# Rotary embedding in a decoder step: the exchange of head halves by DMA instead of matrix products

## The chip, the cores and the metric

One core of one Trainium2 chip runs the whole program. The metric is the device time of one execution in microseconds (us), the median of the runs shown; lower is better.

## The reference, cut to what matters

Two layers of a decoder are computed for 256 prompt tokens and 32 sample tokens (8 sequences of 4), 288 token columns in all, fp32 throughout. A layer is a half-step FFN, a mixing block of three branches (spatial gating, block-sparse attention, memory attention) that all read one combined projection, and a second half-step FFN. The change concerns the queries and keys of the block-sparse attention, which are rotated by position before use: 8 heads of 64 channels, each head split in two halves of 32.

```python
def rope(x, pos):
    hd = x.shape[-1]
    half = hd // 2
    inv = ROPE_THETA ** (-jnp.arange(half, dtype=jnp.float32) * 2.0 / hd)
    ang = pos.astype(jnp.float32)[:, None] * inv[None, :]
    cos = jnp.cos(ang)[None, :, None, :].astype(x.dtype)
    sin = jnp.sin(ang)[None, :, None, :].astype(x.dtype)
    x1, x2 = x[..., :half], x[..., half:]
    return jnp.concatenate([x1 * cos - x2 * sin, x2 * cos + x1 * sin], axis=-1)
...
    h = xn @ w_in
    a_u, a_v, b_q, b_k, b_v, c_q, gates = jnp.split(h, IN_SPLITS, axis=-1)
    q = rope(b_q.reshape(heads), pos)
    k = rope(b_k.reshape(heads), pos)
```

## The kernel before

**Layout and stages.** Activations lie transposed: channels on the 128 partitions, in chunks, and the 288 tokens along the free dimension. Queries and keys have 512 channels each, four chunks of 128x288, so a chunk holds two heads, and a half of a head is a block of 32 partitions. Every weight matrix is streamed from HBM in tiles of 256 columns, in four buffers (two weight slots s of two halves h). ScalarE rounds a loaded half to the fp32r high part (`hi`, L928), VectorE subtracts to get the low part (`lo`, L1303), and TensorE multiplies high by high, high by low and low by high (`tile`, L450, and `part`, L474), three products per chunk and 128 rows. SP issues the weight loads in order; each waits until the low part of the buffer's former contents is done (L1807, L1857).

**The order of the work** is written out by hand for each engine; engines meet only at semaphores, and each engine's queue runs in order. Two result buffers (s = 0 and 1) in PSUM are copied out by ScalarE (`take`, L956), which counts in `evac`; four more banks, numbered by `bank_schedule` (L155), carry transposes and small products.

**The query phase.** TensorE computes the query projection (two tiles at L609 and L617, put by ScalarE into `work[:, 4:6]` and `work[:, 6:8]`, L1089), then the gating values (L622 to L633). VectorE multiplies the queries by the cosine (L1494). Between the halves of the next tile TensorE multiplies each query chunk by a fixed 128x128 matrix `swap` that exchanges the halves of a head with a sign (`rotate`, L569 to L574, called at L623, L624, L627, L628). VectorE multiplies the product by the sine and adds it (`rotate`, L1473 to L1481), then builds block-diagonal queries for the sample group (`own_queries`, L1483) and the block diagonal of the spatial weights (L1504), with the low part of one weight half between the first and the last two rotations (L1497) and two more behind (L1509, L1510).

**The key steps.** 16 steps (L740) transpose four cached key pages each (`page_turn`, L636), with half a projection tile in between, and multiply them by the sample queries (`quad_scores`, L642). GpSimd issues the page loads, four pages (a quad) per step and three quads ahead (`load_quad`, L1923; the loop L1951); between quads it adds squares of the gating values for a layer norm (L1955, L1958), whose sums TensorE takes in steps 1 and 3 (L699 to L705). Transposed pages are copied out by ScalarE (pages 0 and 2) and VectorE (pages 1 and 3). The new keys are projected in steps 0 to 3 and copied out by ScalarE in steps 2 and 4 (`taken`, L1130); VectorE multiplies them by the cosine in steps 3 and 5 (L1591) and rotates them in steps 4 and 6 (L1598, L1602), for which TensorE has two more pairs of `swap` products (L706 to L709). The array `u_T` (`u_t`) is free until ScalarE fills it in steps 6 and 8. The program of GpSimd is written out for both layers.

## Time and profile before

| what | value |
|---|---|
| time, median of 3 runs | 1634.37 us (1634.26 to 1634.77) |
| the profiled execution: time, span | 1636.47 us, 1634.5 us |
| granted TensorE clock, mean of the span | 0.994 |
| DMA traffic | 316.78 MB, 194 GB/s on the mean |

The profile is of one execution. PE is TensorE, PEld its weight loads, DVE is VectorE, ACT ScalarE, POOL GpSimd, SP SyncE; an L number is a line of the kernel. A row of a timeline gives start, length (both us), engine, line, operation, output <- inputs, and how many such instructions follow one another; in brackets, how long the engine had been idle and who ended that. Products overlap in TensorE's pipeline, so a product's length is longer than its share of the time, and start times are the better measure. An fp32 product appears as two instructions.

### The profile page before, as it was taken

Reading aid. Unit: us, or ns where it says so; the run is one execution under the profiler, and the core shown is the slowest. Engines: PE = TensorE matmul, PEld = TensorE weight load, DVE = VectorE, ACT = ScalarE, POOL = GpSimd, SP = SyncE. Lnnn points to the kernel's source line nnn. Section 1 sums busy time; section 2 is a strip of 40 time slices with the busy share of each in tenths; the row PEclk is TensorE's granted clock in tenths of the full one; section 3 lists DMA queues with packets and bytes.
Section 4 is the critical chain, followed back from the end, with each engine's and each line's share of the span. In section 5 each row is a group of like instructions: output and inputs, shape, how many; then the busy total and the mean of one; then the engine's idle time right before and its main releaser. Section 6 shows DMA issues by size and latency. Waiting matters only on the chain.

```text
span 1634.5 us, 34371 instructions
## 1 busy us (share of the span) xinstructions
PE 1602.3 (98%) x13085; PEld 1524.9 (93%) x13085; DVE 938.7 (57%) x1230; ACT 815.8 (50%) x1075; POOL 214.5 (13%) x350
## 2 busy tenths in 40 slices
PE   7999999999999999999999999999999999999996
PEld 6999999998778999999999999999977889999995
DVE  5555556675655566555565555657565556655555
ACT  6756445444635454434476654444455544544343
POOL 1000020332432010000000000113234300100000
PEclk9999999999999999999999999999999999999998
DMA  7555467766876455555555545767678845655552
GB/s 232 157 174 163 145 208 235 255 229 206 278 276 210 145 188 166 165 170 165 169 173 176 155 154 173 264 209 242 217 234 293 269 149 177 190 156 167 162 163 91
DMA packets 253548, 316.78 MB, mean 194 GB/s; under 512 B 12952, under 2 KB 229232, under 8 KB 253424
## 3 DMA queue, kind: packets, MB, share of 16 engines
q1 hardware_dynamic: 225008, 225.87, 44.4%
q0 software_dynamic: 25632, 83.91, 15.0%
q10 hardware_dynamic: 2784, 5.39, 1.0%
q8 instruction: 73, 1.20, 0.3%
q14 instruction: 51, 0.42, 0.1%
HBM read 309.35 MB, written 5.77 MB: 193 GB/s over the span
## 4 chain that ended last, share of the span: by engine, by line
PE 92%; DVE 2%; issue 2%; ACT 1%; DMA 1%; POOL 0%; ACTq 0%; POOLq 0%; SPq 0%; DVEq 0%
PE res L466 44%; PE res L547 17%; PE res L486 16%; PE bank L560 6%; PE bank L648 2%; PE sums L823 2%; PE bank L769 1%; DMA page<-in_cache_v 1%; PE bank L574 0%; PE sums L509 0%; PE bank L795 0%; PE bank L791 0%; POOL work L1904 0%; DVE wlo L1307 0%; DMA xrow<-in_x_prompt 0%
## 5 line engine op out<-in xcount | busy, mean ns | idle before, releaser
L1307 DVE TENSOR_TENSOR wlo<-wraw,whi 128x1024 fp32r<-128x1024 f32 (+1 forms) x452 | 522.4, 1174 | 395.6 <-ACT whi L933 394.3
L933 ACT ACTIVATE whi<-wraw 128x1024 fp32r<-128x1024 f32 (+1 forms) x452 | 443.8, 994 | 279.1 <-PE res L547 143.8
L466 PE MATMUL res<-norm_hi,whi 128*128 128x288 f32 x1632 | 486.1, 298 | 4.7 <-DVE wlo L1307 4.5
L466 PE MATMUL res<-norm_lo,whi 128*128 128x288 f32 x1632 | 483.1, 296 | 0.0
L466 PE MATMUL res<-norm_hi,wlo 128*128 128x288 f32 x1632 | 481.5, 295 | 0.0
L466 PEld LDWEIGHTS res<-norm_hi,whi 128*128 128x128 f32 x1632 | 307.0, 188 | 5.4 <-issue 4.7
L466 PEld LDWEIGHTS res<-norm_hi,wlo 128*128 128x128 f32 x1632 | 308.5, 189 | 0.0
L466 PEld LDWEIGHTS res<-norm_lo,whi 128*128 128x128 f32 x1632 | 307.4, 188 | 0.2
L547 PE MATMUL res<-h_hi,whi 128*128 128x288 f32 x704 | 209.0, 297 | 0.0
L547 PE MATMUL res<-h_lo,whi 128*128 128x288 f32 x704 | 208.1, 296 | 0.0
L547 PE MATMUL res<-h_hi,wlo 128*128 128x288 f32 x704 | 207.5, 295 | 0.0
L486 PE MATMUL res<-norm_hi,whi 128*128 128x288 f32 x544 | 170.8, 314 | 0.0
L1904 POOL TENSOR_TENSOR work<-work 128x576 f32<-128x576 f32 x21 | 36.5, 1738 | 1006.8 <-ACT work L972 1006.6
L486 PE MATMUL res<-norm_lo,whi 128*128 128x288 f32 x544 | 160.5, 295 | 0.0
L486 PE MATMUL res<-norm_hi,wlo 128*128 128x288 f32 x544 | 160.4, 295 | 0.0
L547 PEld LDWEIGHTS res<-h_hi,wlo 128*128 128x128 f32 x704 | 132.7, 188 | 0.0
L547 PEld LDWEIGHTS res<-h_lo,whi 128*128 128x128 f32 x704 | 132.3, 188 | 0.0
L547 PEld LDWEIGHTS res<-h_hi,whi 128*128 128x128 f32 x704 | 132.1, 188 | 0.0
L486 PEld LDWEIGHTS res<-norm_hi,whi 128*128 128x128 f32 x544 | 102.5, 188 | 16.3 <-issue 16.1
L1107 ACT ACTIVATE kT<-bank 128x512 f32<-128x512 f32 x80 | 47.8, 597 | 123.3 <-PE bank L560 123.3
L486 PEld LDWEIGHTS res<-norm_lo,whi 128*128 128x128 f32 x544 | 102.7, 189 | 0.2
L486 PEld LDWEIGHTS res<-norm_hi,wlo 128*128 128x128 f32 x544 | 102.3, 188 | 0.0
(209 smaller groups left out, 2130.1 us busy)
## 6 DMA issues: line engine op xcount, KB each, us to landing
wraw<-in_ffn_w SPq DMA_DIRECT2D x244, 512.0 KB, 4.2
wraw<-in_w_in SPq DMA_DIRECT2D x96, 512.0 KB, 4.8
page<-in_cache_k POOLq DMA_DIRECT2D x128, 256.0 KB, 4.6
page<-in_cache_v POOLq DMA_DIRECT2D x128, 256.0 KB, 5.0
wraw<-in_ffn_w SPq DMA_DIRECT2D x32, 384.0 KB, 3.0
wraw<-in_w_mem_kv SPq DMA_DIRECT2D x16, 512.0 KB, 3.4
page<-in_cache_mem_k POOLq DMA_DIRECT2D x32, 256.0 KB, 4.7
page<-in_cache_mem_v POOLq DMA_DIRECT2D x32, 256.0 KB, 3.5
```

Of the source, the lines that this page charges most:

```text
L466: mm = pe.matmul(res[:, 2 * s + c, 0:n], w_, m_, start=h == 0 and k == 0 and i == 0, stop=h == 1 and k == kh - 1 and i == 2)
L486: mm = pe.matmul(res[:, 2 * s + c, 0:T], w_, m_, start=h == 0 and k == 0 and i == 0, stop=h == 1 and k == kh - 1 and i == 2)
L547: mm = pe.matmul(res[:, 2 * ps + c, 0:T], w_, m_, start=part == 0 and h == 0 and k == 0 and i == 0, stop=part == 2 and h == 1 and k == kh ...
L560: mm = pe.transpose(d, i_, ident[0:i_.shape[0], 0:i_.shape[0]])
L648: mm = pe.matmul(out(bb), q_[:, c, bb, :], kTb[bb][:, c, :], start=c == 0, stop=c == 3)
L769: mm = pe.matmul(bk(nm)[:, qt * 256:(qt + 1) * 256], lhs, rhs, start=True, stop=True)
L823: mm = pe.matmul(bk(nm)[32 * bb:32 * bb + 32, :], PT[:, j, 32 * bb:32 * bb + 32], page[slot(V0 + v, bb)][:], start=j == 0, stop=j == 7)
L933: act.activation(whi[u][:, 0:kh, :], wraw[u][:, 0:kh, :], ACT.Copy).then_inc(hi_done[u], 1)
L1107: act.activation(kTb[bb][:], bk(f"{name}_{bb}")[:, :].rearrange("p (c m) -> p c m", c=4), ACT.Copy)\
L1307: dve.tensor_tensor(wlo[u][:, 0:kh, :], wraw[u][:, 0:kh, :], whi[u][:, 0:kh, :].bitcast(F32), ALU.subtract)\
L1904: a = pool.tensor_tensor(work[:, 0:2, :], work[:, 0:2, :], work[:, 2 * g:2 * g + 2, :], ALU.add)
```

## The change

The matrix `swap`, its eight products per layer, their banks and the VectorE operations on them go. The sine table gets the sign (minus in the first half of a head). GpSimd has a function `exchange(n)` for the two halves of the queries (n = 0, 1) and of the keys (n = 2, 3): it waits for ScalarE's copy of that projection tile, and for the keys until VectorE has read the array's former contents, and then issues four DMAs that copy two chunks of `work` into `u_t`, each of the four blocks of 32 partitions from the block beside it in its head. Each DMA moves 32 partitions x 2304 B. Exchanges 0 and 1 stand before the loads of page quad 3, exchange 2 before quad 6 (and before the addition that is issued there), exchange 3 before quad 8. VectorE waits for all four DMAs of an exchange (`ld_half`), multiplies the exchanged two chunks by the sine in one operation, and adds them in another. The cosine product of the queries is cut into two halves, the first of which moves ahead of the last low part of the pair before. The first low part of the key phase, `lo(0, 0, 8, 1)`, moves behind the block diagonals. ScalarE's wait at step 10 becomes waits at steps 6 and 8, before it overwrites `u_t`.

```diff
@@ -47,8 +47,8 @@
 UP = FF // W
 
 
-C_ID, C_ONE, C_EPS, C_SWAP = 0, 128, 256, 264
-C_COS, C_SIN = C_SWAP + 128, C_SWAP + 128 + T
+C_ID, C_ONE, C_EPS, C_COS = 0, 128, 256, 264
+C_SIN = C_COS + T
 C_CAUSAL = C_SIN + T
 C_NEWMASK = C_CAUSAL + 512
 C_TRIL = C_NEWMASK + 64
@@ -67,17 +67,12 @@
     p = np.arange(P)
     c[:, C_ID:C_ID + P] = np.eye(P)
     c[:, C_ONE:C_ONE + P] = 1.0
-    for m in range(P):
-        if m % HD < HD // 2:
-            c[m + HD // 2, C_SWAP + m] = -1.0
-        else:
-            c[m - HD // 2, C_SWAP + m] = 1.0
     pos = np.concatenate([np.arange(SEQ), np.tile(PAST + np.arange(DEC_T), DEC_B)]).astype(np.float32)
     half = HD // 2
     inv = np.float32(10000.0) ** (-np.arange(half, dtype=np.float32) * np.float32(2.0) / np.float32(HD))
     ang = pos[None, :] * inv.astype(np.float32)[p % half][:, None]
     c[:, C_COS:C_COS + T] = np.cos(ang.astype(np.float64))
-    c[:, C_SIN:C_SIN + T] = np.sin(ang.astype(np.float64))
+    c[:, C_SIN:C_SIN + T] = np.sin(ang.astype(np.float64)) * np.where(p % HD < half, -1.0, 1.0)[:, None]
     key = np.arange(SEQ)
     for qt in range(2):
         c[:, C_CAUSAL + 256 * qt:C_CAUSAL + 256 * qt + 256] = np.where(key[None, :] <= p[:, None] + P * qt, 0.0, NEG)
@@ -129,7 +124,7 @@
 PAIRS = 56
 RES = 48
 SUMS = 5
-STEPS = 51
+STEPS = 56
 HEADS = 12
 KSTEPS = 16
 GATE_STEPS = 12
@@ -156,8 +151,8 @@
 
     pro = [(f"in{t}_{q}", q) for t in range(3) for q in range(2)] + [("gainT", 2)]
     layer = [(f"mt{f}", f % 3) for f in range(4)] + [("mk0", 0), ("mk1", 1), ("wmT", 2), ("mv0", 0), ("mv1", 1)]
-    layer += [("rotq0", 0), ("rotq1", 1), ("rotq2", 0), ("rotq3", 1), ("rep", 2)]
-    side = {4: ["rotk0", "rotk1"], 6: ["rotk2", "rotk3"], 8: ["vn0", "vn1"], 9: ["vn2"], 10: ["sgu0", "sgu1"],
+    layer.append(("rep", 2))
+    side = {8: ["vn0", "vn1"], 9: ["vn2"], 10: ["sgu0", "sgu1"],
             11: ["sgu2", "sgu3"], 12: ["k0", "k1"], 13: ["k2", "v2"], 14: ["pT0_0", "pT1_0"], 15: ["v0", "v1"]}
     for i in range(KSTEPS):
         layer += [(f"kT{i}_{bb}", bb % 2) for bb in range(4)] + [(nm, b) for b, nm in enumerate(side.get(i, []))]
@@ -307,7 +302,6 @@
 
     ident = cst[:, C_ID:C_ID + P]
     ones = cst[:, C_ONE:C_ONE + P]
-    swap = cst[:, C_SWAP:C_SWAP + P]
     epsc = cst[:, C_EPS:C_EPS + 1]
 
 
@@ -370,6 +364,7 @@
     ld_gain = sem("ld_gain")
     ld_x = [sem(f"ld_x{i}") for i in range(3)]
     ld_page = sem("ld_page_ids")
+    ld_half = [sem(f"ld_exchanged_{n}") for n in ("q0", "q1", "k0", "k1")]
     ld_sw = sem("ld_sgu_w")
     ld_sb = sem("ld_sgu_b")
     out_mem, out_vn, out_k, out_v, out_y = (sem(n) for n in ("out_mem", "out_vn", "out_k", "out_v", "out_y"))
@@ -566,14 +561,6 @@
             b = bk(name)
             transposes(name, (L,), [src[:, c, c0:c0 + m] for c in range(4)], [b[0:m, c * P:(c + 1) * P] for c in range(4)])
 
-        def rotate(L, which, c):
-
-            name = f"rot{which}{c}"
-            free(name, L)
-            o = 4 if which == "q" else 0
-            pe.matmul(bk(name)[:, 0:T], swap, work[:, o + c, :], start=True, stop=True).then_inc(filled_of(name), 1)
-
-
         pe.wait_ge(ld_const, 16)
         for t in range(3):
             pe.wait_ge(ld_x[t], 16)
@@ -619,13 +606,7 @@
                 rows(f"mv{t}", L, work, t)
 
 
-            part(0, 0, 8, normed)
-            rotate(L, "q", 0)
-            rotate(L, "q", 1)
-            part(0, 1, 8, normed)
-            pe.wait_ge(evac[1], r[1].at())
-            rotate(L, "q", 2)
-            rotate(L, "q", 3)
+            tile(0, 8, normed)
             wait(empty("wmT", L))
             free("rep", L)
             pe.matmul(bk("rep")[0:NS, 0:16].rearrange("p (g i) -> p g i", g=4), cst[:, C_REP:C_REP + NS],
@@ -677,7 +658,7 @@
                 nm = f"newS_{G}"
                 if G == 0:
                     pe.wait_ge(sum_read, nsum.at(1))
-                    pe.wait_ge(rot_ready, L * 8 + 8)
+                    pe.wait_ge(rot_ready, L * 4 + 4)
                 free(nm, L)
                 for c in range(4):
                     for bb in range(4):
@@ -703,10 +684,6 @@
                 elif i == 3:
                     pe.wait_ge(ch_added, L * 2 + 2)
                     sum_channels(lnsq)
-                elif i in (4, 6):
-                    pe.wait_ge(evac[(i - 4) // 2], r[(i - 4) // 2].at(-1 if i == 4 else 0))
-                    rotate(L, "k", i - 4)
-                    rotate(L, "k", i - 3)
                 elif i == 8:
                     pe.wait_ge(vn_ready, L + 1)
                     rows("vn0", L, gv, 0)
@@ -1037,7 +1014,7 @@
                     split_high(g, lambda k: slice(G_FFN1 + k, G_FFN1 + k + 1))
             hi(s, h, 8, 0)
             square(i)
-        act.dma_start(cst[:, C_SWAP:C_ALL], A["const"][:, C_SWAP:C_ALL]).then_inc(ld_rest, 16)
+        act.dma_start(cst[:, C_COS:C_ALL], A["const"][:, C_COS:C_ALL]).then_inc(ld_rest, 16)
 
         with repeat(act, DEPTH, {cur: PAIRS, r[0]: RES, r[1]: RES, nsum: SUMS, nf: 4, soft_n: HEADS,
                                  silu_n: 2 * UP, xr: 8}) as L:
@@ -1139,9 +1116,8 @@
                     act.activation(lnsq[:], gv[:], ACT.Square, scale=SGU ** -0.5).then_inc(xc_sq, 1)
                 hi(u // 2, u % 2, 4 if i > 12 and u >= 2 else 8, 1)
                 key_copy(f"kT{i}", 2, i)
-                if i == 10:
-                    wait(fill("rotq3", L))
-                    act.wait_ge(rot_ready, L * 8 + 4)
+                if i in (6, 8):
+                    act.wait_ge(rot_ready, L * 4 + i // 2)
                 if i in taken:
                     take(*taken[i])()
                 if u == 3:
@@ -1461,24 +1437,27 @@
             for g in (1, 2, 3):
                 normal_low(g)
             pair(FULL)
-            pair(FULL)
+            cosb = cst[:, C_COS:C_COS + T].unsqueeze(1)
+
+            def queries(s):
+                dve.wait_ge(evac[s], r[s].at(3))
+                step(dve.tensor_tensor(qk[:, 2 * s:2 * s + 2, :], work[:, 4 + 2 * s:6 + 2 * s, :], cosb.broadcast_to([P, 2, T]),
+                                       ALU.mult))
+            pair(FULL, None, lambda: queries(0))
 
 
             wait(fill("wmT", L))
             tril = cst[:, C_TRIL:C_TRIL + P].unsqueeze(1).broadcast_to([P, 4, P])
             dve.tensor_tensor(wmT[:], bk("wmT")[:, :].rearrange("p (g i) -> p g i", g=4), tril, ALU.mult)\
                 .then_inc(emptied_of("wmT"), 1)
-            cosb = cst[:, C_COS:C_COS + T].unsqueeze(1)
-
-            def rotate(which, c):
-                nm, o = f"rot{which}{c}", 0 if which == "q" else 4
-                wait(fill(nm, L))
-                tmp = rtmp[c % 2]
-                if o + c >= 2:
-                    dve.wait_ge(rot_ready, L * 8 + (o + c - 1))
-                dve.tensor_tensor(tmp[:], bk(nm)[:, 0:T], cst[:, C_SIN:C_SIN + T], ALU.mult).then_inc(emptied_of(nm), 1)
-                wait(empty(nm, L))
-                dve.tensor_tensor(qk[:, o + c, :], qk[:, o + c, :], tmp[:], ALU.add).then_inc(rot_ready, 1)
+
+            def rotate(n):
+
+                half, two = u_t[:, n % 2 * 2:n % 2 * 2 + 2, :], qk[:, 2 * n:2 * n + 2, :]
+                dve.wait_ge(ld_half[n], L * 64 + 64)
+                sinb = cst[:, C_SIN:C_SIN + T].unsqueeze(1).broadcast_to([P, 2, T])
+                step(dve.tensor_tensor(half, half, sinb, ALU.mult))
+                dve.tensor_tensor(two, two, half, ALU.add).then_inc(rot_ready, 1)
 
             def own_queries(G):
                 for c in range(4):
@@ -1489,16 +1468,11 @@
                                               1.0, None, ALU.mult)
                 i.then_inc(qbd_ready, 1)
 
-            dve.wait_ge(evac[0], r[0].at(3))
-            dve.wait_ge(evac[1], r[1].at(3))
-            step(dve.tensor_tensor(qk[:, 0:4, :], work[:, 4:8, :], cosb.broadcast_to([P, 4, T]), ALU.mult))
-            rotate("q", 0)
-            rotate("q", 1)
-            lo(0, 0, 8, 1)
-            rotate("q", 2)
-            rotate("q", 3)
+            rotate(0)
+            queries(1)
             step(dve.memset(qbd[:], 0.0))
-            dve.wait_ge(rot_ready, L * 8 + 4)
+            rotate(1)
+            dve.wait_ge(rot_ready, L * 4 + 2)
             own_queries(0)
             wait(fill("rep", L))
             for g in range(4):
@@ -1506,6 +1480,7 @@
                 msk = cst[0:NS, C_BD:C_BD + NS].rearrange("p (b i) -> p b i", b=DEC_B)
                 i = dve.tensor_tensor(bd[:, g, :].rearrange("p (b i) -> p b i", b=DEC_B), src, msk, ALU.mult)
             i.then_inc(emptied_of("rep"), 1)
+            lo(0, 0, 8, 1)
             lo(0, 1, 8, 1)
             lo(1, 0, 8, 1)
             r[0].n += 4
@@ -1597,12 +1572,10 @@
                                            cosb.broadcast_to([P, 2, T]), ALU.mult))
                 elif i == 4:
                     block_scores(0)
-                    rotate("k", 0)
-                    rotate("k", 1)
+                    rotate(2)
                 elif i == 6:
                     step(dve.tensor_tensor(gv[:], gv[:], rstd[:].unsqueeze(1).broadcast_to([P, 4, T]), ALU.mult))
-                    rotate("k", 2)
-                    rotate("k", 3)
+                    rotate(3)
                 elif i == 7:
                     for k in range(4):
                         a = dve.tensor_scalar(gv[:, k, :], gv[:, k, :], gains[:, ds(L * 4 + (G_LNG + k), 1)],
@@ -1623,7 +1596,7 @@
                     dve.wait_ge(ld_sb, L * 16 + 16)
                     dve.wait_ge(evac[0], r[0].at(2))
                     dve.wait_ge(evac[1], r[1].at(2))
-                    dve.wait_ge(rot_ready, L * 8 + 8)
+                    dve.wait_ge(rot_ready, L * 4 + 4)
                     spatial(0)
                     spatial(1)
                 elif i == 11:
@@ -1822,7 +1795,7 @@
                 nk = DOWN_NK[part]
                 load(t % 2, wt[w2][L][:, 8 * part:8 * part + nk, g * W:(g + 1) * W], nk)
 
-        sp.dma_start(cst[:, 0:C_SWAP], A["const"][:, 0:C_SWAP]).then_inc(ld_const, 16)
+        sp.dma_start(cst[:, 0:C_COS], A["const"][:, 0:C_COS]).then_inc(ld_const, 16)
         sp.dma_start(xrow[0][:], A["x_prompt"][0, 0:P, :]).then_inc(ld_x[0], 16)
         sp.dma_start(xrow[1][:], A["x_prompt"][0, P:2 * P, :]).then_inc(ld_x[1], 16)
         sp.dma_start(xrow[2][0:NS, :], A["x_sample"].rearrange("b t d -> (b t) d")).then_inc(ld_x[2], 16)
@@ -1948,7 +1921,23 @@
                     e = slot(quad, bb)
                     pool.dma_start(page[e][:], src).then_inc(page_loaded[e], 16)
             add_squares()
+
+            def exchange(n):
+
+                s, c = n % 2, 4 - n // 2 * 4 + n % 2 * 2
+                pool.wait_ge(evac[s], L * RES + MIX_TILES + n // 2 * 2)
+                if n >= 2:
+                    pool.wait_ge(rot_ready, L * 4 + n - 1)
+                for p0 in range(0, P, HD // 2):
+                    p1 = p0 ^ (HD // 2)
+                    pool.dma_start(u_t[p0:p0 + HD // 2, 2 * s:2 * s + 2, :], work[p1:p1 + HD // 2, c:c + 2, :])\
+                        .then_inc(ld_half[n], 16)
             for quad in range(QUADS):
+                if quad == 3:
+                    exchange(0)
+                    exchange(1)
+                if quad in (6, 8):
+                    exchange(quad // 2 - 1)
                 if quad == 4:
                     pool.wait_ge(evac[1], L * RES + MIX_TILES + 1)
                     pool.wait_ge(out_v, L * 32 + 16)
```

## Rows read from the trace of the kernel before

**Rows 1.** Busy time of each engine, share of the span, instructions.

```profile
PE 1602.3 (98%) x13085; PEld 1524.9 (93%) x13085; DVE 938.7 (57%) x1230; ACT 815.8 (50%) x1075; POOL 214.5 (13%) x350
```

**Rows 2.** The chain that ended last, shares of the span by engine.

```profile
PE 92%; DVE 2%; issue 2%; ACT 1%; DMA 1%; POOL 0%; ACTq 0%; POOLq 0%; SPq 0%; DVEq 0%
```

**Rows 3.** TensorE's waits, 240 to 420 us: for whom, total us, times, longest.

```profile
PE bank L648 <- DVE scores L1527: 0.4, 1, 0.4
```

**Rows 4.** Line 574, the rotation products: lengths in ns, first and last start.

```profile
L574 PE MATMUL bank<-work,consts x32: 405/406/407, 274.1 to 1130.1; 128*128 128x288 f32 x32
```

**Rows 5.** Timeline of TensorE at the first pair of rotation products.

```profile
273.99 0.29 PE L486 MATMUL res<-norm_hi,wlo 128*128 128x288 f32 x1
274.12 1.13 PE L574 MATMUL bank<-work,consts 128*128 128x288 f32 x4
...
275.23 0.29 PE L486 MATMUL res<-norm_lo,whi 128*128 128x288 f32 x1
275.36 0.29 PE L486 MATMUL res<-norm_hi,wlo 128*128 128x288 f32 x1
```

**Rows 6.** Timeline of TensorE, second pair and first page transposes.

```profile
278.28 1.13 PE L574 MATMUL bank<-work,consts 128*128 128x288 f32 x4
279.35 0.24 PE L631 MATMUL bank<-sgu_wT,consts 128*32 128x16 f32 x2
...
286.01 1.04 PE L560 MATMUL bank<-consts,page 128*128 128x128 f32 x8
...
288.46 1.04 PE L560 MATMUL bank<-consts,page 128*128 128x128 f32 x8
```

**Rows 7.** Timeline of TensorE, key steps 2 and 4.

```profile
301.60 1.04 PE L560 MATMUL bank<-consts,page 128*128 128x128 f32 x8
...
304.15 1.08 PE L648 MATMUL bank<-kT,q_blockdiag 128*32 128x128 f32 x32
...
314.73 1.04 PE L560 MATMUL bank<-consts,page 128*128 128x128 f32 x8
...
318.26 1.08 PE L648 MATMUL bank<-kT,q_blockdiag 128*32 128x128 f32 x32
```

**Rows 8.** Page loads: a burst of four from 308.9; then 262 to 420 us.

```profile
L1949 POOL DMA_DIRECT2D page<-in_cache_k x4: 536/536/553, 309.0 to 310.6; - x4
...
DMA to landing us min/median/max: 2.8/4.5/6.4
...
DMA to landing us min/median/max: 2.7/4.2/8.5
```

**Rows 9.** Timeline of GpSimd, key steps 0 to 3.

```profile
287.25 1.13 POOL L1949 DMA_DIRECT2D page<-in_cache_k  x2 [41.76 <-PE bank L560]
...
302.84 1.13 POOL L1949 DMA_DIRECT2D page<-in_cache_k  x2 [1.34 <-PE bank L560]
307.67 1.42 POOL L1958 TENSOR_TENSOR ln_square<-ln_square 128x576 f32<-128x576 f32 x1 [3.70 <-ACT ln_square L1139]
```

**Rows 10.** Timeline of ScalarE, query phase.

```profile
270.27 0.65 ACT L960 ACTIVATE work<-res 128x576 f32<-128x576 f32 x1 [2.08 <-PE res L466]
...
283.07 1.06 ACT L933 ACTIVATE whi<-wraw 128x1024 fp32r<-128x1024 f32 x1 [2.04 <-PE res L466]
```

**Rows 11.** Timeline of VectorE, query phase and key steps 3 and 4.

```profile
273.04 0.68 DVE L1469 TENSOR_TENSOR sgu_wT<-bank,consts 128x512 f32<-128x512 f32 x1
...
283.63 1.45 DVE L1487 TENSOR_SCALAR q_blockdiag<-qk_T 64x16 f32<-64x16 f32 x8
285.12 0.47 DVE L1507 TENSOR_TENSOR sgu_blockdiag<-bank,consts 32x32 f32<-32x32 f32 x4
285.52 2.33 DVE L1307 TENSOR_TENSOR wlo<-wraw,whi 128x1024 fp32r<-128x1024 f32 x2
...
310.69 0.74 DVE L1596 TENSOR_TENSOR qk_T<-work,consts 128x576 f32<-128x576 f32 x1
...
317.13 0.69 DVE L1529 TENSOR_REDUCE stat<-scores 128x2 f32<-128x512 f32 x1
```

## Prediction

> **What bounds the kernel now.** I read the busy shares first: TensorE is busy for 98% of the span [rows 1], no other engine for more than 57%. Busy alone proves nothing, so next the chain that ended last: 92% of it is TensorE, and VectorE, ScalarE and the DMAs share some 4% [rows 2]. Then TensorE's own waits, in the stretch of layer 0 that holds all four pairs of rotation products: the longest is 0.4 us, behind a VectorE read of scores [rows 3]. So every microsecond taken off TensorE's stream there comes off the time, until another engine falls so far behind that TensorE waits for it. The rest of the working is about that "until".
>
> **What goes: the products.** Line 574 stands with 32 instructions [rows 4]: each of the 16 fp32 products is two of them, and they come in pairs of products, four pairs in a layer, eight in all. Their 406 ns overlap in the pipeline, so the price is read from start times. At the first pair the last column product before it starts at 273.99, the pair at 274.12, and the stream is back in its step of 0.13 from 275.23 on [rows 5]; without the pair the instruction of 275.23 would start at 274.12 + 0.13 = 274.25. A pair costs 0.98, a third of it the slow change back. Behind the second pair stands another fp32 product (L631), which starts 1.07 later than the pair [rows 6]. For the key pairs I compare two steps: from the second page transposes to the scores a step without any extra product takes 304.15 - 301.60 = 2.55, one with a rotation pair 318.26 - 314.73 = 3.53 [rows 7]. Again 0.98. Sum: 8 x 0.98 = **7.8 us**; with 1.07 for the two pairs before L631 it would be 8.0. That the step without products runs at 2.55 with no wait also says that the engines around it can follow the shorter step.
>
> **What comes: 32 DMAs on GpSimd's queue.** An exchange is four DMAs of 32 partitions x 2304 B (74 KB), four exchanges in a layer. Issuing: four page loads in a row cost GpSimd 0.54 each [rows 8], so an exchange is 2.1 us of GpSimd and 16 issues are 8.6 us in a layer. What is queued behind them there:
> - The exchanges of the queries come before the loads of page quad 3. GpSimd has sat idle for 41.76 us before these [rows 9], waiting for the first page transposes; both exchanges lie inside, so nothing behind them moves.
> - The first key exchange comes after quad 5 and before the addition L1958, whose sum TensorE multiplies in step 3. Quad 5 is out at 302.84 + 1.13 = 303.97, the addition starts at 307.67, having waited 3.70 for ScalarE [rows 9]: 2.1 us of issuing fit, with 1.5 to spare. The second comes after quad 7, and GpSimd then waits for transposes again.
>
> Landing is the number that the trace does not have: nothing copies SBUF to SBUF here. The nearest rows are those four page loads in one burst on the same queue, 256 KB each: 2.8 to 6.4 us, median 4.5. The fastest page of this phase took 2.7 us, the slowest 8.5 [rows 8]. I take **4.5** (same queue, same burst of four, with more bytes than here), and keep 2.7 and 8.5 as ends.
>
> **Who waits for the landing.** Only VectorE, in order, and only one of the four exchanges is tight: the second half of the queries. Its source is ScalarE's copy that ends at 270.27 + 0.65 = 270.92 [rows 10], before any product that goes, so this time stays. GpSimd issues from 271.0, the fourth DMA at 272.7; landed at 277.2. VectorE meanwhile masks the spatial weights until 273.7, rotates the first half (landed long before; two operations of 128x576 at 0.74 each [rows 11]) until 275.2, does the cosine product of the second half and the clearing, and then waits until 277.2. Behind that wait on VectorE are the rotation (1.5), the own queries (1.45), the block diagonals (0.47) and three low parts of weights at 1.17 [rows 11], of which the first has moved from before the second half of the queries to behind the block diagonals; the last also needs ScalarE's high part, which ends at 283.07 + 1.06 less the 2.0 that TensorE is ahead by then, 282.1 [rows 10]. So the low parts end at 280.6 + 3.5 = 284.1.
> When does TensorE need that? Its first page transposes move from 286.01 to 284.0, the next pair from 288.46 to 286.45 [rows 6], and the fourth page goes into the bank that VectorE's copy of the second page empties, some 0.5 behind that. With the copy at 0.7, VectorE must be free of the low parts by 286.2: 2.1 us to spare, or a landing at 279.3, which is 6.6 us after the fourth issue. 4.5 is free, so is the 6.4 of the burst; at 8.5 the landing is at 281.2, 1.9 late in a layer, **3.8 us** in two. A landing faster than 4.5 gains nothing, since then ScalarE's high part is last.
> The low part that moved also releases a weight load on SP: it ends at 280.6 + 1.2 = 281.8, and ScalarE takes that buffer's next contents only in key step 1, behind the transposes of 286.45, so the load has more than 5 us. The key exchanges are easy: issued by 304.1 in the new times, landed by about 308; VectorE reaches the first key rotation when its block scores end, 317.13 + 0.69 - 2.0 = 315.8 [rows 11].
>
> **Edits at nothing.** VectorE's own work: per layer 17 operations go and 10 come, over the same 5,760 columns (1152 + 16 x 288 against 10 x 576), beside TensorE throughout. The cosine product of the first queries goes into a gap where VectorE waits for ScalarE before the last low part. ScalarE's wait in step 10 becomes waits in steps 6 and 8 on rotations that VectorE ends two steps earlier; if one were late, the activation of that step and the high part of the next would queue behind it. SP's first constant load keeps its size, ScalarE's gets 64 KB smaller. The 2.4 MB of exchanges stand against 316.78 MB moved.
>
> **Sum.** 7.8 off, nothing back. The profiled execution has a span of 1634.5 and a time of 1636.47, 2.1 above the median of the runs; I take the difference from the median: 1634.37 - 7.8 = **1626.6**.
>
> **A rule of the skill that speaks against the change.** The burst row says that DMAs of one queue overlap: four issued within 2.1 us, and the slowest landed 6.4 after its issue [rows 8]. The Trainium skill, "DMA: Bandwidth & Descriptors", section "Rules for kernel authors", says of two transfers to disjoint partition halves "Don't bother — they serialize", and would have one transfer over all partitions. By the fit that the page has in its section "Anatomy of one DMA — SWDGE (gpsimd) path" (2.0 us and the bytes at 436 GB/s; an estimate of 2.2 for 74 KB) four in a row would land 8.7 after the first issue, at 279.7, 0.4 late in a layer, and the sum would be 7.0: 1627.4. No run here shows an exchange yet.
>
> **The rivals.**
> - *Late landing, chance 0.10.* The second query exchange meets the two 512 KB writes of the memory keys and values and the weight loads, and lands like the slowest page. For: ScalarE issues these writes just behind the copy that releases the exchange. Against: the burst stayed at 6.4. Price 3.8: 1630.4.
> - *Serial exchanges, slower, chance 0.05.* The four DMAs go one at a time, each with a whole landing: 4 x 4.5 = 18 after 271.0 is 289.0, 9.7 later than free. VectorE stands at the second query rotation, TensorE at the first kT bank. Twice 9.7 less 7.8 is 11.6: 1646. If the key rotations were held too (18 after 302.0 is 4 past 315.8), it would be more. It becomes a loss once the landing is 3.9 past 279.3, at 283.2, 12 us after the first issue. Against: the burst row.
> - *Nothing gained, chance 0.08.* Another chain sets the pace of the steps (page, transpose, copy, scores), and the time freed turns into TensorE waits: 1634.4. For: two copies per step sit close behind the transposes. Against: rows 7, a step without products at full pace.
>
> **How the numbers follow.** The forecast has the remaining 0.77. Its own spread: a vanished wait of 0.4 in each layer and 1.07 for the L631 pairs would bring 1625.6, less some noise 1625.2. Upwards the range takes in the late landing with a little room: 1631.0. A measurement of this kernel can tell about 0.2%, 3.3 us, from no change; forecast and late landing are faster (0.87, less 0.01 for a hold that I don't see: 0.86), nothing gained is the same (0.08), serial exchanges and that 0.01 are slower (0.06).
>
> **What would show it.** Right: no line 574, the key steps 4 and 6 at 2.55 from transposes to scores, no new TensorE wait on VectorE's kT copy between the query phase and step 1, exchanges landing 3 to 6 us after issue, VectorE idle for about 1 us before the second query rotation. Wrong: VectorE idle there for over 3 us and TensorE waiting at the first kT banks (late or serial), TensorE waiting for the sum of L1958 (issuing dearer than 0.54, above 0.9), or key steps that keep 3.5.

## The result, and the profile after

The changed kernel takes **1622.80 us**, median of 4 runs (1621.78 to 1626.50), beside 1634.57 for the kernel before on the same chip. The ratio is 0.993 [0.9918, 0.9943]: 11.4 us less, between 9.3 and 13.4. The forecast was 1626.6, 7.8 less, with 1625.2 as its lower end: right in sign, too small in size. A second series of the same kernel, further down, has 0.9938 [0.9924, 0.9951], 10.1 less. So what has to be explained is 10 to 11.5 us, of which the forecast has 7.8.

Busy times and the chain that ended last, of the page after (they answer to [rows 1] and [rows 2]):

```profile
PE 1591.8 (98%) x13053; PEld 1520.2 (94%) x13053; DVE 937.4 (58%) x1216; ACT 815.9 (50%) x1075; POOL 230.5 (14%) x382
...
PE 96%; DVE 2%; issue 1%; ACT 0%; DMA 0%; POOLq 0%; SPq 0%; DVEq 0%; ACTq 0%
```

TensorE has lost its 32 instructions and is still busy for 98%. But look at the chain: before, it had 92% TensorE, 2% "issue" and 1% DMA; now TensorE has 96% and the DMA share is gone. Removing products alone doesn't take a DMA out of the chain. That is the first sign that something else went too.

TensorE in key steps 2 and 4, its timeline after (it answers to [rows 7]):

```profile
299.78 1.04 PE L555 MATMUL bank<-consts,page 128*128 128x128 f32 x8
302.33 1.08 PE L629 MATMUL bank<-kT,q_blockdiag 128*32 128x128 f32 x32
...
312.91 1.04 PE L555 MATMUL bank<-consts,page 128*128 128x128 f32 x8
315.47 1.08 PE L629 MATMUL bank<-kT,q_blockdiag 128*32 128x128 f32 x32
```

Step 4, from transposes to scores, now takes 2.56, as step 2 does (2.55); it was 3.53.

The exchanges, by their source line: how many, ns of one issue (min/median/max), who waited for them, and the time from issue to landing:

```profile
L1933 POOL DMA_DIRECT2D u_T<-work x32: 496/498/513, 263.6 to 1106.3; - x32
...
  DVE u_T L1459: 0.4, 1
DMA to landing us min/median/max: 1.9/4.2/6.5
```

An issue takes 0.50 (forecast 0.54), a landing 4.2 in the median (4.5). Of all eight exchanges VectorE waited for one, for 0.4 us, in layer 1.

VectorE after, layer 0, from the first query rotation to the first key copy (it answers to [rows 11]):

```profile
273.81 0.75 DVE L1459 TENSOR_TENSOR u_T<-u_T,consts 128x576 f32<-128x576 f32 x1
...
275.27 0.75 DVE L1444 TENSOR_TENSOR qk_T<-work,consts 128x576 f32<-128x576 f32 x1
276.20 0.48 DVE L1473 MEMSET q_blockdiag<- 128x512 f32 x1 [0.17 <-DVE qk_T L1444]
276.72 0.76 DVE L1459 TENSOR_TENSOR u_T<-u_T,consts 128x576 f32<-128x576 f32 x1
...
280.18 3.47 DVE L1283 TENSOR_TENSOR wlo<-wraw,whi 128x1024 fp32r<-128x1024 f32 x3
285.34 0.69 DVE L1492 COPY kT<-bank 128x512 f32<-128x512 f32 x1 [1.69 <-PE bank L555]
```

The second rotation starts at 276.72 (forecast 277.2) without a wait (forecast: about 1 us idle), the low parts end at 283.65 (284.1), and then VectorE waits 1.69 for TensorE, not TensorE for VectorE. GpSimd after (it answers to [rows 9]):

```profile
271.31 1.96 POOL L1933 DMA_DIRECT2D u_T<-work  x4 [5.73 <-ACT work L937]
285.46 1.18 POOL L1922 DMA_DIRECT2D page<-in_cache_k  x2 [12.20 <-PE bank L555]
...
302.16 1.98 POOL L1933 DMA_DIRECT2D u_T<-work  x4
305.85 1.42 POOL L1947 TENSOR_TENSOR ln_square<-ln_square 128x576 f32<-128x576 f32 x1 [1.71 <-ACT ln_square L1116]
```

Behind the query exchanges GpSimd still sits idle for 12.20 us, and behind the first key exchange the addition still waits 1.71 for ScalarE (forecast 1.5 to spare). So in the stretch that the forecast went through, all but VectorE's idle microsecond came as written, and that one costs nothing.

**Where the rest came from.** I aligned the two TensorE streams: for each matmul, its start in the kernel before less its start in the kernel after. The difference grows by 0.97 at each of the eight pairs of products, 7.8 in all. It then grows by 5.5 us in layer 0 (0.4 of it at one wait for VectorE's softmax values, a step that the two kernels of the fourth series show too) and by 1.2 in layer 1 where TensorE multiplies the value pages (L823 before, L800 after): a stretch that the change doesn't touch. These steps make up 14.5 of the 14.7 by which the two spans differ, so the granted clock (0.994 before, 0.996 after) has no visible part in it. TensorE's waits there over the whole span, kernel before, matmuls and then weight loads (us in total, times, longest):

```profile
PE sums L823 <- DMA page<-in_cache_v: 2.6, 2, 2.0
...
PEld sums L823 <- DMA page<-in_cache_v: 6.9, 9, 2.9
```

and the kernel after, in which only the weight loads still wait:

```profile
PEld sums L800 <- DMA page<-in_cache_v: 1.2, 3, 0.7
```

The values are loaded and used in quads of four pages, 16 in a layer (0 to 15). The worst is quad 12 of layer 0. TensorE and GpSimd of the kernel before around it:

```profile
460.30 2.27 PE L823 MATMUL sums<-page,past_probs_T 128*32 128x512 f32 x12
464.55 1.55 PE L823 MATMUL sums<-page,past_probs_T 128*32 128x512 f32 x4 [1.98 <-DMA page<-in_cache_v]
```

```profile
447.14 2.31 POOL L1949 DMA_DIRECT2D page<-in_cache_v  x4 [9.16 <-PE sums L823]
455.03 0.54 POOL L1949 DMA_DIRECT2D page<-in_cache_v  x1 [5.58 <-PE sums L823]
458.17 4.11 POOL L1949 DMA_DIRECT2D page<-in_cache_v  x7 [2.61 <-issue]
```

GpSimd issues the first load of quad 12 at 455.03 and then **stands still for 2.61 us** before the second; "issue" means that the profile shows nothing that it waits for. The last page lands at 465.01; TensorE's first product on the quad starts at 461.18, 3.83 us earlier. In the kernel after, GpSimd goes through (quad 11, then quads 12 and 13):

```profile
441.94 2.33 POOL L1922 DMA_DIRECT2D page<-in_cache_v  x4 [8.19 <-issue]
449.29 4.68 POOL L1922 DMA_DIRECT2D page<-in_cache_v  x8 [5.02 <-PE sums L800]
```

and quad 12 is 0.23 late. The 8.19 ahead of quad 11 is mostly a wait for a free buffer, though the view says "issue": TensorE released the buffer only 1.18 us before the load (0.63 before it in the kernel before). So the questions for the chip: is it the products alone that give 7.8, what moves the standstill, and is there anything else?

### The profile page after: what moved, and what is told of

Same layout as the page of the kernel before. It is cut to its first block, busy times and chain, and to the rows that moved or that the text cites. A ratio compares the mean times of both kernels' runs of the same rounds, so it can differ in the third digit from the quotient of the medians.

```text
span 1619.8 us, 34245 instructions
## 1 busy us (share of the span) xinstructions
PE 1591.8 (98%) x13053; PEld 1520.2 (94%) x13053; DVE 937.4 (58%) x1216; ACT 815.9 (50%) x1075; POOL 230.5 (14%) x382
## 4 chain that ended last, share of the span: by engine, by line
PE 96%; DVE 2%; issue 1%; ACT 0%; DMA 0%; POOLq 0%; SPq 0%; DVEq 0%; ACTq 0%
PE res L461 47%; PE res L542 17%; PE res L481 17%; PE bank L555 7%; PE bank L629 2%; PE sums L800 2%; PE bank L746 1%; PE sums L504 1%; PE bank L772 0%; PE bank L768 0%; PE bank L636 0%; PE bank L652 0%; DVE kT L1492 0%; PE sums L629 0%; DMA xrow<-in_x_prompt 0%
## 5 line engine op out<-in xcount | busy, mean ns | idle before, releaser
L461 PEld LDWEIGHTS res<-norm_hi,wlo 128*128 128x128 f32 x1664 | 314.5, 189 | 0.0
L1492 DVE COPY kT<-bank 128x512 f32<-128x512 f32 x80 | 55.2, 690 | 74.4 <-PE bank L555 73.6
```

What stands on the lines that cost most here:

```text
L461: mm = pe.matmul(res[:, 2 * s + c, 0:n], w_, m_, start=h == 0 and k == 0 and i == 0, stop=h == 1 and k == kh - 1 and i == 2)
L1492: dve.tensor_copy(kTb[bb][:], bk(f"{name}_{bb}")[:, :].rearrange("p (c m) -> p c m", c=4))\
```

## The experiments

Loads are counted from 0 in each layer: 64 key pages, 64 value pages, 32 memory pages. The first load of value quad 12 is 112, its second 113. In the table at the end of this part, "late" is worked out from the records: for each value quad, the landing of its last page less the start of TensorE's first matmul on it, where positive, summed over both layers.

**First series: code place or shorter stream.** My first idea was that GpSimd's standstill depends on where it stands in its instruction stream.

*Products out* (TensorE's rotation products go, VectorE multiplies the chunk itself, so the halves aren't exchanged, and keeps its order; GpSimd as before):

```
-            rotate(L, "q", 0)
-            rotate(L, "q", 1)
...
-                dve.tensor_tensor(tmp[:], bk(nm)[:, 0:T], cst[:, C_SIN:C_SIN + T], ALU.mult).then_inc(emptied_of(nm), 1)
-                wait(empty(nm, L))
+                step(dve.tensor_tensor(tmp[:], work[:, 4 - o + c, :], cst[:, C_SIN:C_SIN + T], ALU.mult))
```

> The kernel before without the 16 rotation products: VectorE multiplies the unrotated chunk itself by the sine, so the exchange of head halves is left out; GpSimd's program is that of before. The changed kernel won 11.8 us, of which the aligned starts of TensorE's products in the two traces put 7.8 at the products and the rest at two or three waits for value pages behind the key steps. Theory A (the rest comes from GpSimd's program: its longer code moved the place at which GpSimd waits for its next block of instructions, out of the loads of value quad 12): the products alone give 7.8, 1626.8 with 1 us to either side, and the wait for quad 12 stays. Theory B (the rest comes from TensorE's shorter stream, which changes how page loads and weight loads meet): 1622.8, and the wait goes.

Measured: 1627.36, ratio 0.9948 [0.9934, 0.9962], 8.5 less. The standstill stays at the same load:

```profile
449.93 0.54 POOL L1936 DMA_DIRECT2D page<-in_cache_v  x1 [5.58 <-PE sums L813]
453.07 5.29 POOL L1936 DMA_DIRECT2D page<-in_cache_v  x9 [2.61 <-issue]
```

and one wait is new: with the old order on VectorE, the key copy is late once the products are gone (TensorE's timeline; 0.67 in each layer against the kernel after):

```profile
286.39 0.60 PE L560 MATMUL bank<-consts,page 128*128 128x128 f32 x4
287.50 0.63 PE L560 MATMUL bank<-consts,page 128*128 128x128 f32 x4 [0.51 <-DVE kT L1504]
```

*Padding* (the kernel before, 18 semaphore increments in each layer of GpSimd's stream ahead of quads 3, 6 and 8), *both* (products out and padding), and *after, shifted* (the kernel after with 238 increments at the start):

```
+                for _ in range({3: 9, 6: 4, 8: 5}.get(quad, 0)):
+                    pool.sem_inc(padded, 1)
```

> The kernel before with 18 more instructions per layer in GpSimd's program, semaphore increments that nobody waits for, 9 before quad 3, 4 before quad 6 and 5 before quad 8: as many as the exchanges add there by the trace. Products and rotation stay. Theory A: the wait for value quad 12 goes, 1634.6 - 4 = 1630.6 (1629.6 to 1632). Theory B: nothing changes, 1634.6.

> Both edits together: the products out (the exchange of halves is left out) and the 18 instructions per layer in GpSimd's program, no DMAs. Theory A: the two gains add, 1622.8, the time of the changed kernel, and the 32 exchange DMAs and the reordered VectorE work cost nothing. Theory B: 1622.8 as well, but then the run without the padding gives the same. If the exchanges cost something in the changed kernel, this one is faster than 1622.8 by it.

> The changed kernel with 238 semaphore increments in GpSimd's program ahead of the layers, where it idles for 176 us. In the trace of before GpSimd's long gaps stand at its instructions 396, 661 and 909, some 256 apart; 238 more bring the second load of value quad 12 of layer 0 back onto such a place (414 + 238 = 652). Theory A: that load waits some 2.6 us again and TensorE 2.5 to 3.6 for the page: 1625.3 to 1626.4. Theory B: 1622.8.

Measured: padding 1634.98, ratio 0.9999 [0.999, 1.0008]; both 1627.28, 0.995 [0.9936, 0.9964]; after, shifted 1624.22, 0.993 [0.9916, 0.9944]. Padding changes nothing, and the standstill is at the very same load:

```profile
454.67 0.54 POOL L1950 DMA_DIRECT2D page<-in_cache_v  x1 [5.58 <-PE sums L824]
457.82 5.29 POOL L1950 DMA_DIRECT2D page<-in_cache_v  x9 [2.61 <-issue]
```

The place in the code falls as a cause. So does the shorter stream: without products the quad is still 3 us late, and *both*, which both theories put at 1622.8, stays at 1627.28. *After, shifted* lies between the two theories' times, but its trace has no standstill at quad 12.

**Second series: the transfers.** *Small transfers* (kernel before):

```
+            for j in range(16):
+                pool.dma_start(spare[0:32, 0 + 16 * L + j:0 + 16 * L + j + 1], cst[0:32, 0:1]).then_inc(spared, 16)
             add_squares()
```

> The kernel before, products and all, with 16 small transfers per layer (32 numbers each) issued by GpSimd in its idle time before the layer's page loads. In the kernel before, GpSimd stands still for 2.61 us (455.57 to 458.17) inside the loads of value quad 12, with no wait shown; that quad then lands 3.83 us after TensorE wants it. The padded kernels had it at the same load (its 114th transfer), whatever the number of instructions; the kernel after has it at its 125th, the first load of value quad 11. Theory C (the standstill comes with the number of transfers issued, counted by their rows, and costs only where it falls on a quad without slack): the standstill moves to the 125th transfer, quad 11, which has 7 us of slack; TensorE's wait for quad 12 in layer 0 shrinks by 2.6 us; 1632.3 us (1631.3 to 1633.3), 2.6 less than the kernel before. Theory D (the transfers move nothing; the quads come in time because TensorE or VectorE is placed otherwise): as the kernel before, 1635.0.

*Exchange out* and *exchange tiny* (kernel after; in both VectorE multiplies the halves that weren't exchanged):

```
-                dve.wait_ge(ld_half[n], L * 64 + 64)
...
-                step(dve.tensor_tensor(half, half, sinb, ALU.mult))
+                o = 4 - n // 2 * 4 + n % 2 * 2
+                step(dve.tensor_tensor(half, work[:, o:o + 2, :], sinb, ALU.mult))
...
-                    pool.dma_start(u_t[p0:p0 + HD // 2, 2 * s:2 * s + 2, :], work[p1:p1 + HD // 2, c:c + 2, :])\
-                        .then_inc(ld_half[n], 16)
+                    pass
```

```
-                step(dve.tensor_tensor(half, half, sinb, ALU.mult))
+                o = 4 - n // 2 * 4 + n % 2 * 2
+                step(dve.tensor_tensor(half, work[:, o:o + 2, :], sinb, ALU.mult))
...
-                    pool.dma_start(u_t[p0:p0 + HD // 2, 2 * s:2 * s + 2, :], work[p1:p1 + HD // 2, c:c + 2, :])\
+                    pool.dma_start(u_t[p0:p0 + HD // 2, 2 * s:2 * s + 1, 0:1], work[p1:p1 + HD // 2, c:c + 1, 0:1])\
                         .then_inc(ld_half[n], 16)
```

> The kernel after with the exchanges left out: VectorE multiplies the chunk's own, unexchanged halves (so the rotation is not computed), in the order of the kernel after. Theory C: the standstill goes back to the 114th transfer, the second load of value quad 12 in layer 0; 2.6 us more than the kernel after, 1625.4 us (1624.2 to 1626.4). Theory D: as the kernel after or a little less, 1622.5 (1621.5 to 1623.3), as nothing waits for the exchanges. What it is below the kernel of the first call without products and with the old order on VectorE (1627.4) is the price of that order, by the aligned traces 1.3 us.

> The kernel after with exchanges of one number per partition: the same 16 transfers per layer, of 32 rows of 4 bytes in the place of 2304; VectorE still waits for them and multiplies the unexchanged halves (so the rotation is not computed). Theory C: as the kernel after, 1622.8 us (1621.8 to 1623.8), the standstill at the 125th transfer as there; the size of the exchanges costs nothing. If the bytes of the exchanges (288 KB each, 1.2 MB in a layer) delay weights or pages, it is below 1621.8.

*More transfers* (kernel after, 45 of the small ones once, ahead of the layers):

> The kernel after with 45 small transfers (32 numbers each) issued by GpSimd at the start, in its idle time. Theory C, with a row count that fits both kernels (9 units a page load, 3 an exchange, up to 1020): the standstill comes earlier by 135 units, 15 page loads, and falls on the second load of value quad 7 in layer 0, which has 0.05 us of slack in the kernel after: TensorE waits there for 2.5 us more; 1625.3 us (1624.3 to 1626.3). Theory D: as the kernel after, 1622.8.

Measured: small transfers 1636.55, ratio 1.0015 [1.0006, 1.0023]; exchange out 1626.53, 0.9951 [0.9939, 0.9964]; exchange tiny 1624.15, 0.9936 [0.9924, 0.9949]; more transfers 1624.81, 0.994 [0.9927, 0.9953].

Exchange out and exchange tiny came out 0.1 and 0.4 above their ranges. Two expectations fell. Sixteen transfers ahead of the page loads don't move the standstill off quad 12 of layer 0, and they put a second one on quad 12 of layer 1 (small transfers, GpSimd's timeline), which is 3.05 late there instead of 1.65; the kernel gets slower:

```profile
454.65 0.54 POOL L1952 DMA_DIRECT2D page<-in_cache_v  x1 [5.02 <-PE sums L825]
457.73 5.29 POOL L1952 DMA_DIRECT2D page<-in_cache_v  x9 [2.54 <-issue]
...
1252.43 0.54 POOL L1952 DMA_DIRECT2D page<-in_cache_v  x1 [5.55 <-PE sums L825]
1255.52 6.57 POOL L1952 DMA_DIRECT2D page<-in_cache_v  x11 [2.55 <-issue]
```

And 45 transfers at the start leave the long standstill where it is in the kernel after. So it isn't the sum of what GpSimd has issued. But without the exchanges the standstill is back at quad 12 (exchange out),

```profile
451.34 0.54 POOL L1922 DMA_DIRECT2D page<-in_cache_v  x1 [5.58 <-PE sums L800]
454.48 5.89 POOL L1922 DMA_DIRECT2D page<-in_cache_v  x10 [2.61 <-issue]
```

and with exchanges of four bytes a row it is gone (exchange tiny), 2.4 us faster:

```profile
450.67 4.69 POOL L1923 DMA_DIRECT2D page<-in_cache_v  x8 [5.02 <-PE sums L800]
```

So the transfers move it, by where they stand and not by their bytes. One rule fits the standstills of 2.4 to 2.6 us in the traces: one comes at the load that follows 113 page loads without another transfer among them, and then every 102. The exchanges end 32 loads into a layer; 32 + 113 is load 145, the second memory value page. There the kernel after has 2.39 us of idle time that the kernel before doesn't have, though the profile names a TensorE product as its end. GpSimd at loads 144 to 147 of layer 0, before and after:

```profile
496.77 1.06 POOL L1949 DMA_DIRECT2D page<-in_cache_mem_v  x2 [2.65 <-PE bank L560]
499.22 1.06 POOL L1949 DMA_DIRECT2D page<-in_cache_mem_v  x2 [1.39 <-PE bank L560]
```

```profile
487.58 0.54 POOL L1922 DMA_DIRECT2D page<-in_cache_mem_v  x1 [2.65 <-PE bank L555]
490.51 1.59 POOL L1922 DMA_DIRECT2D page<-in_cache_mem_v  x3 [2.39 <-PE bank L555]
```

**Third series: one transfer; the limit of the landing; a better share of the quads.** *One transfer* (kernel before):

```
+                if quad == 8:
+                    pool.dma_start(spare[0:32, L:L + 1], cst[0:32, 0:1]).then_inc(spared, 16)
                 load_quad(quad)
```

> The kernel before, products and all, with one small transfer (32 numbers) per layer, issued by GpSimd just ahead of its ninth quad of page loads (where the kernel after has its last exchange). Theory E, read from the ten traces so far: GpSimd stands still for 2.4 to 2.6 us at the load that follows 113 page loads with no other transfer among them, and after that every 102; any other transfer starts the count anew, so the exchanges ahead of the ninth quad (32 loads in) put it at load 32 + 113 = 145 of each layer, the second load of the first memory values, and off the second load of value quad 12 (load 113). Then one transfer does what sixteen did: no standstill at load 113, one at load 145 in both layers, TensorE's wait for quad 12 in layer 0 shorter by 2 to 2.6 us, and 1632.4 us (1631.4 to 1633.4) beside 1634.6 for the kernel before. Theory F (the sum of what was issued decides, sixteen transfers as much as five page loads): one transfer moves the standstill by less than a load; it stays at load 113, 1634.6.

Measured: 1634.67, ratio 0.9992 [0.9983, 1.0001]: at most 2.8 us less, perhaps nothing. The trace shows why it is little (GpSimd, quad 12 and the memory values of layer 0):

```profile
455.75 0.54 POOL L1952 DMA_DIRECT2D page<-in_cache_v  x1 [5.58 <-PE sums L825]
457.28 4.11 POOL L1952 DMA_DIRECT2D page<-in_cache_v  x7 [1.00 <-issue]
...
495.43 0.54 POOL L1952 DMA_DIRECT2D page<-in_cache_mem_v  x1 [2.65 <-PE bank L562]
498.36 1.59 POOL L1952 DMA_DIRECT2D page<-in_cache_mem_v  x3 [2.39 <-PE bank L562]
```

The long standstill has gone to load 145, as the rule says, but a short one of 1.00 stays at quad 12 (and one of 1.55 at load 87 of layer 1). The quad is 1.77 late instead of 3.83. So moving the standstill with one transfer, in the kernel before, gains nothing that is clear of the noise.

*Second exchange late* (kernel after):

```
                     exchange(0)
+                    for j in range(24 * L, 24 * L + 24):
+                        pool.dma_start(spare[0:32, j:j + 1], cst[0:32, 0:1]).then_inc(spared, 16)
                     exchange(1)
```

> The kernel after with 24 small transfers (32 numbers each) between the first and the second query exchange on GpSimd's queue: at 0.50 us each they push the second exchange's first issue from 271.3 to 277.6 us and its landing from 276.6 to 282.9. By the prediction's limit (a landing at 279.3 is the latest that TensorE does not feel) that is 3.6 us too late in each layer: 7.2 more than the kernel after, 1630 us (1628 to 1632). If the second query exchange has more room than that, it is as the kernel after, 1623.

Measured: 1631.88, ratio 0.9975 [0.9965, 0.9985], 6.0 above the kernel after of the same series. It landed at 282.7. VectorE, and then TensorE:

```profile
282.81 0.76 DVE L1461 TENSOR_TENSOR u_T<-u_T,consts 128x576 f32<-128x576 f32 x1 [5.09 <-DMA u_T<-work]
...
286.27 3.47 DVE L1285 TENSOR_TENSOR wlo<-wraw,whi 128x1024 fp32r<-128x1024 f32 x3
```

```profile
287.62 0.37 PE L483 MATMUL res<-norm_hi,whi 128*128 128x288 f32 x1 [1.38 <-DVE wlo L1285]
...
290.49 0.63 PE L557 MATMUL bank<-consts,page 128*128 128x128 f32 x4 [0.61 <-DVE kT L1494]
```

By the aligned streams TensorE loses 2.4 in layer 0 and 4.3 in layer 1. A landing at 282.7 that costs 2.4 puts the limit at 280.3. In layer 1 it landed at 1077.87, which is 283.7 in the times of layer 0 (the first exchanges are issued 794.2 apart), and 4.3 less than that is 279.4. This execution runs 1.0 behind the kernel after (its first exchange is issued at 264.63 for 263.60), so in the times of the kernel after the limit is 278.4 to 279.3. The prediction had 279.3. The first to wait isn't the fourth transpose, though, but the product behind the low part that the change moved.

*Values spread* (kernel after), and the *kernel after again* beside it:

```
-VALUES = [(0, 1), (1, 1), (2, 1), (3, 2), (4, 1), (5, 2), (7, 1), (8, 2), (9, 2), (10, 2), (11, 1)]
+VALUES = [(0, 1), (1, 1), (2, 2), (3, 1), (4, 1), (5, 2), (7, 2), (8, 2), (9, 1), (10, 2), (11, 1)]
```

> The kernel after with another share of the value quads among the steps of the heads: two at step 2 and one at step 3 (there one and two), two at step 7 and one at step 9 (there one and two). A quad's slots are loaded again for the third quad behind it; quads 7, 12 and 14, which have -0.2 to 0.1 us of slack in layer 0 of the kernel after and -1.1 to 0.7 in layer 1 (and -0.5 to -2.1 in other runs of it), then have 3 us or more. If waits for value pages are what is left of that loss: 1.5 us less than the kernel after of the same call (0.3 to 3), about 1621.3 us. If the quads also cover waits of the heads' own steps, moving them opens others, and it is as the kernel after or slower.

> The kernel after, unchanged, beside the others of this call: 1623 us (1622 to 1625).

Measured: spread 1621.43 (1620.87 to 1623.49), ratio 0.9914 [0.99, 0.9927]; after again 1625.86 (1622.89 to 1628.14), 0.9938 [0.9924, 0.9951]. No quad is late any more. Quads 7, 12 and 14, which were, have 2.0 us or more to spare; the nearest is now quad 11 of layer 0, with 0.07. The runs lie closer together, and it is the fastest of all. The gain over the kernel after is 3.9 us by the ratios, where 1.5 was expected; the kernel after is itself 3 us above its first series and above its expectation here.

**Fourth series: the same spread in the kernel before.** With no late quad on either side, only the products and VectorE's order are left between the two kernels.

> The kernel before, products and all, with the value quads shared among the steps as in the spread kernel of the call before (two at step 2, one at step 3, two at step 7, one at step 9). In ten traces TensorE's waits for the pages of value quads 7, 12 and 14, both layers, sum to 4.5 to 7.5 us where GpSimd's standstill falls on quad 12 without the exchanges, and to 1.1 to 3.8 us in the kernel after and its variants. Theory: the part of the gain that the prediction missed is this and nothing else. Then without these waits the kernel before is 5 us faster (3 to 7), 1629.5 us, and the kernel after with the same spread stands 7.8 below that (6.5 to 9), the price of the products alone. Rival (the exchanges or VectorE's order gain something outside of these waits too): the spread kernel before is 1632 or more, or the two spread kernels stand 10 or more apart.

> The kernel after with the same spread, unchanged from the call before, beside it: 1621.5 us (1620.5 to 1623).

Measured: before, spread 1629.76 (1628.72 to 1631.29), 0.9969 [0.9959, 0.998]; after, spread 1622.35 (1620.79 to 1622.82), 0.9921 [0.9908, 0.9935]. The two stand 7.4 apart by the medians, 7.8 by the ratios (0.0048 of 1635.38), 7.7 by the spans (1628.1 and 1620.4); the aligned streams step by 0.96 or 0.97 at each of the eight pairs. And GpSimd in the kernel before with the spread:

```profile
445.01 2.91 POOL L1949 DMA_DIRECT2D page<-in_cache_v  x5 [7.64 <-PE sums L823]
450.52 1.74 POOL L1949 DMA_DIRECT2D page<-in_cache_v  x3 [2.61 <-issue]
```

The standstill is still there, of the same length, at the same load. It costs nothing now, since quad 12 has slack. So it was never the standstill alone, but the standstill on a quad that is needed at once.

| kernel | late, us | time, us |
|---|---|---|
| before | 7.5 | 1634.57 |
| small transfers | 6.9 | 1636.55 |
| products out | 5.3 | 1627.36 |
| one transfer | 5.0 | 1634.67 |
| padding / both | 4.9 / 4.8 | 1634.98 / 1627.28 |
| second exchange late | 4.7 | 1631.88 |
| exchange out | 4.5 | 1626.53 |
| more transfers / after, shifted | 3.8 / 3.6 | 1624.81 / 1624.22 |
| exchange tiny | 3.1 | 1624.15 |
| after / after again | 1.4 / 1.1 | 1622.80 / 1625.86 |
| the three spread kernels | 0 | 1621.43, 1629.76, 1622.35 |

"Late" is of one profiled execution; the times are medians of several, from five series, in which the kernel before had 1634.57 to 1635.87.

## Why the prediction was right, and where it failed

- **The products: right.** 8 x 0.98 was forecast; 0.97 at each pair in the streams, 7.4 to 7.8 between the spread kernels.
- **The exchanges are free: right.** Issues of 0.50 for 0.54, landings of 4.2 for 4.5, the second query exchange at 276.61 against a limit of 279.3. That the limit is real was shown by going past it, and it lies at 278.4 to 279.3; the first waiter there was named wrong. The margin is thin: that exchange landed between 4.0 and 6.8 after its first issue in the kernel after and its variants with whole exchanges in place, and the limit is 7.1 to 8.0 after it. Exchanges of four bytes a row gave no less than whole ones, so their bytes cost nothing that these runs can tell.
- **VectorE's order: right, and needed.** The prediction let it cost nothing. With the old order and no products TensorE waits 0.67 in each layer; the new one has 1.69 us to spare there.
- **Late landing, serial exchanges, nothing gained: none of the three.** The four transfers of an exchange overlap: issued from 263.60 to 265.08, the last landed at 267.02. The Trainium skill's rule ("DMA: Bandwidth & Descriptors", "Rules for kernel authors") that such transfers serialize isn't borne out here: the prediction, with that rule and the page's fit, estimated 8.7 for four in a row, and they took 3.4 on quiet queues and 5.3 for the second query exchange. The slowest of this trace, among page loads, took 8.0 (1104.85 to 1112.83).
- **The step that failed is the sum, "7.8 off, nothing back".** It took TensorE's waits from 240 to 420 us alone [rows 3] and let all behind that be carried along unchanged. The value pages behind it are no rigid load: their transfers go through the queue into which the change puts 32 new ones. For that queue the prediction asked what stands behind the exchanges and finds its time, and found rightly that nothing there is delayed. It didn't ask where that queue already held TensorE up. Both stood in the views of the kernel before: 1% DMA in the chain [rows 2], and the waits of line 823 in the list over the whole span.
- **What it measured.** In the five kernels whose standstill falls on quad 12 of layer 0 alone (before, products out, padding, both, exchange out) the quads are 5.4 us late in the mean; in the five with the exchanges in their places and on time (after, after again, shifted, tiny, more transfers) 2.6. That is 2.8 more to gain, and 7.8 + 2.8 = 10.6 lies between the two series, 10.1 and 11.4. In the two profiled executions themselves it is 7.5 less 1.4. That the late value pages are the whole rest, as far as the noise lets one tell, is shown by the spread kernels: with none late, 7.4 to 7.8 is left.

**What stays open.** Why GpSimd stands still, and why a transfer of another kind moves it. The rule of 113 and 102 loads is read from these traces; shorter standstills are not in it, such as 1.15 at load 82 of layer 1 in the kernel after, or the 1.00 and 1.55 in the kernel with one transfer. These last two come where the count would be without that transfer (113, and 145 + 102, which is load 87 of the next layer), so a transfer may shorten a standstill and not only start the count anew; that wasn't tested. VectorE as the cause is unlikely. The Trainium skill, "SBUF — State Buffer", section "SBUF: two separate sides", warns that some VectorE operations keep GpSimd from writing its descriptors. The trace doesn't bear it out here: during the standstill from 455.57 to 458.17 VectorE is idle for 0.61 us (457.24 to 457.85) and GpSimd doesn't go on, and in other places the two run side by side with issues of 0.54. What a quad's lateness is without any standstill also changes from run to run (quad 12 of layer 0: 0.2 to 1.7 in the kernel after and its variants), and the part of the 2.8 that is landing and not standstill wasn't told apart. The nearest test is exchange tiny against exchange out, 2.4 less; one transfer in the kernel before showed no clear gain.

## What to carry to other kernels

A change that puts new transfers on a queue should be priced on everything that this queue feeds, over the whole span, also where nothing has to wait longer: list the bottleneck's waits of the whole kernel first, and say for each whether the change can make it longer or shorter. Where loads have a fixed depth of buffers, look for the one that is needed right after it was asked for: spreading the use of the groups so that none is needed the moment it lands (here a change of four entries in a list) was worth 5 us in the kernel before, and a standstill on the queue then costs nothing. And to price one part of a change, remove the waits that scatter on both sides before comparing.

## What was not expected of the hardware

- A transfer from SBUF to SBUF of 32 partitions by 2304 B landed 1.9 to 2.0 us after its issue on quiet queues, four of them in one burst, and 4.2 to 6.5 beside page loads.
- Issuing it costs GpSimd 0.50 us, and a page load of 256 KB 0.54: a transfer 3.5 times as large costs 8% more to issue.
- GpSimd's standstill of 2.4 to 2.6 us inside a run of loads, at the same load whatever the code around it: load 113 in every kernel without another transfer behind the first load, load 145 with the last one 32 loads in.
